# A long convolution inside a two-block model: transforms of half length over even and odd times

## The reference, cut to what matters

```python
h = jnp.sin(f1 * (z @ w1 + b1))
h = jnp.sin(f2 * (h @ w2 + b2))
h = h @ w3                                  # filters: 2 orders x 2 directions x 1024 channels
kern = concatenate([h_fwd, zeros(1), h_bwd[:0:-1]])      # after a decay window
kf = rfft(kern)

def long_conv(u, kf, bias):                 # u: 256 times x 1024 channels
    uf = rfft(u, n=512)
    return irfft(uf * kf, n=512)[:256] + u * bias

z   = hx1 * long_conv(hv, kf[order 0], bias[0])
y_a = hx2 * long_conv(z,  kf[order 1], bias[1])
```

## Time and profile before

| | |
|---|---|
| time, median of 3 runs | 2843.58 us (2842.61 to 2844.23) |
| the profiled execution's own time | 2843.16 us |
| its span, first to last instruction | 2840.9 us |
| PE busy | 2735.8 us (96%) |
| DVE busy | 1570.4 us (55%) |
| ACT busy | 1170.1 us (41%) |
| mean granted clock of PE | 0.985 |
| the Hyena mixer, from its first transpose to `br_b`'s first product | 1762.88 to 1884.55 us |

### The profile page before, as it was taken

The page is one execution under the profiler, slowest core; times in us unless marked ns, Lnnn a source line. Parts: engine busy times, 40 slices in busy tenths (PEclk is TensorE's granted clock), DMA queues, the critical chain, the costliest instruction groups (busy, mean ns, idle before and its releaser), DMA issues. The chain is left out here.

```text
span 2840.9 us, 53209 instructions
## 1 busy us (share of the span) xinstructions
PE 2735.8 (96%) x21454; PEld 2628.4 (93%) x21454; DVE 1570.4 (55%) x1868; ACT 1170.1 (41%) x1345; POOL 64.6 (2%) x59
## 2 busy tenths in 40 slices
PE   8999999999999999999999997989999999999998
PEld 8999898999988988999999994479999999999998
DVE  6445666564455665667654444556565555554443
ACT  5333465443343554433344442024354444443332
POOL 0000011010000000100000000000010000000000
PEclk9999999999999999999999997999999999999999
DMA  6555322545544334555555550025555555555553
GB/s 216 173 177 177 131 93 75 166 157 178 171 148 135 121 109 142 180 198 178 177 181 189 188 181 23 15 70 186 189 167 189 186 184 185 177 193 185 185 182 123
DMA packets 123699, 445.96 MB, mean 157 GB/s; under 512 B 13594, under 2 KB 15925, under 8 KB 123440
## 3 DMA queue, kind: packets, MB, share of 16 engines
q1 hardware_dynamic: 122208, 438.82, 47.0%
q0 software_dynamic: 1360, 5.27, 0.6%
HBM read 441.94 MB, written 2.10 MB: 156 GB/s over the span
## 5 line engine op out<-in xcount | busy, mean ns | idle before, releaser
L1611 PE MATMUL PS<-XH,hi 128*128 128x256 f32 (+1 forms) x5152 | 1466.0, 285 | 37.3 <-DVE lo L891 20.5
L1613 PE MATMUL PS<-XH,lo 128*128 128x256 f32 (+1 forms) x5152 | 1460.7, 284 | 0.0
L1612 PE MATMUL PS<-XL,hi 128*128 128x256 f32 (+1 forms) x5152 | 1460.1, 283 | 0.0
L891 DVE TENSOR_TENSOR lo<-raw,hi 128x1024 fp32r<-128x1024 f32 x728 | 898.8, 1249 | 853.9 <-ACT hi L467 842.7
L467 ACT ACTIVATE hi<-raw 128x1024 fp32r<-128x1024 f32 x728 | 762.0, 1057 | 1007.2 <-PE PS L1613 966.9
L1611 PEld LDWEIGHTS PS<-XH,hi 128*128 128x128 f32 x5152 | 975.1, 189 | 42.0 <-issue 28.4
L1612 PEld LDWEIGHTS PS<-XL,hi 128*128 128x128 f32 x5152 | 975.3, 189 | 0.1
L1613 PEld LDWEIGHTS PS<-XH,lo 128*128 128x128 f32 x5152 | 974.6, 189 | 0.0
L1673 PE MATMUL PS<-XH,hi 128*128 128x256 f32 (+1 forms) x768 | 229.4, 299 | 2.6 <-DVE XL L946 2.6
L1675 PE MATMUL PS<-XH,lo 128*128 128x256 f32 (+1 forms) x768 | 220.3, 287 | 0.0
L1674 PE MATMUL PS<-XL,hi 128*128 128x256 f32 (+1 forms) x768 | 219.7, 286 | 0.0
(11 more groups left out here) (329 smaller groups left out, 1602.9 us busy)
## 6 DMA issues: line engine op xcount, KB each, us to landing
raw<-stream SPq DMA_DIRECT2D x828, 512.0 KB, 3.6
H<-h_in SPq DMA_DIRECT2D x4, 544.0 KB, 8.2
y_win<-windows POOLq DMA_DIRECT2D x2, 1024.0 KB, 5.5
out<-H SPq DMA_DIRECT2D x4, 512.0 KB, 3.5
dftm<-dft POOLq DMA_DIRECT2D x1, 1024.0 KB, 5.8
w<-w POOLq DMA_DIRECT2D x2, 512.0 KB, 6.8
ml_m<-mask_ml POOLq DMA_DIRECT2D x1, 512.0 KB, 3.9
a_m<-masks_a POOLq DMA_DIRECT2D x1, 272.0 KB, 6.4
```

The source lines that it names most:

```text
L891: dve.tensor_tensor(lo[s][:, :], raw[s][:, :], hi[s][:, :].bitcast(F32), ALU.subtract)\
L1611: pe.matmul(PS[:, bank, 0:n], w_hi, x_hi, start=start, stop=False)
L1612: pe.matmul(PS[:, bank, 0:n], w_hi, x_lo, start=False, stop=False)
L1613: return pe.matmul(PS[:, bank, 0:n], w_lo, x_hi, start=False, stop=stop)
```

## The change

The transforms go to half length. Times are split into even and odd ones, 128 each, and the 256 bins into 128 low ones and their mirrors. The even times give a half spectrum A. Then the odd times are added in the same PSUM bank, which gives the low bins A + B. A mirror bin is A - B, and it is made as twice the even part less the sum: ACT copies A out (`first_half`) before the odd product starts, ACT copies the sum (`low_half`), and DVE makes 2A - (A + B) (`high_half`). Both spectra, of the filter and of the input, are now taken this way, so `spectra_product` reads SBUF only; it has two operations more, which form sum and difference over the mirrored bins (`y_Z`) for an inverse of half length. `y_back` has again 16 products, of 128 columns, and writes every second column of its bank.

The two directions of the filter are stacked in 128 rows: w3 lies with one direction in rows 0 to 63 and the other in rows 64 to 127, and `h2T` has a second copy with the lower rows negated, so that one product gives the sum and another the difference (`filter_rows` on DVE makes the rows, and zeroes the first time of the second direction). `windowed` is then two products with the window. The second layer of the filter's network works on 128 rows.

The units are reordered: `v % 2` is the half of the channels and `v // 2` the order. The first `y_filters` moves from ahead of the mLSTM's last part to behind the first turn, the windows come in one load, w3 in one load instead of two. In three places `root_read` moves PE's wait for the square root from chunk 5 of the product to chunk 7 (`kv`; `w2` and `gate_up` in the same way). The diff, cut to its core; of the removed functions, which are printed above, only some lines are kept:

```diff
+y_banks = {"input": 0, "sum": 2, "difference": 4, "filter": 4, "output": 6}
...
-    w3_halves = w3.rearrange("p (b h n) -> h p b n", h=2, n=512)
     gp.wait_ge(S("m_vt"), 4)
-    gp.dma_start(w3_0[:, :, :], w3_halves[0]).then_inc(S("w3_landed0"), 16)
+    gp.dma_start(y_w3[:, :, :], w3).then_inc(S("w3_landed"), 16)
     gp.wait_ge(S("m_num"), 2 * MH)
-    gp.dma_start(y_win[:, :, :, :], windows[:, :, :, 0:512]).then_inc(S("window_landed0"), 16)
-    gp.wait_ge(S("m_out"), MH)
-    gp.dma_start(w3_1[:, :, :], w3_halves[1]).then_inc(S("w3_landed1"), 16)
-    gp.wait_ge(S("y_windowed"), 4 * 2)
-    gp.dma_start(y_win[:, :, :, :], windows[:, :, :, 512:1024]).then_inc(S("window_landed1"), 16)
+    gp.dma_start(y_win[:, :, :, :], windows).then_inc(S("window_landed"), 16)
...
+        def turned(v):
+            act.wait_ge(S("y_ut"), v + 1)
+            if v:
+                act.wait_ge(S("y_us"), v)
+            act.activation(y_U[:, :, :], PS[:, 0:2, :], ACT.Copy).then_inc(S("y_u"), 1)
+        def first_half(name, dst, bank, v):
+            act.wait_ge(S(f"y_{name}A"), v + 1)
+            if v:
+                act.wait_ge(S("y_prod"), v)
+            act.activation(dst[:, :, 1, :], PS[:, bank:bank + 2, :], ACT.Copy).then_inc(S(f"y_{name}a"), 1)
+        def low_half(name, dst, bank, v):
+            act.wait_ge(S(f"y_{name}s"), v + 1)
+            act.activation(dst[:, :, 0, :], PS[:, bank:bank + 2, :], ACT.Copy).then_inc(S(f"y_{name}l"), 1)
         turned(0)
+        first_half("k", y_K, y_banks["filter"], 0)
+        first_half("u", y_V, y_banks["input"], 0)
+        low_half("k", y_K, y_banks["filter"], 0)
+        for v in range(4):
+            low_half("u", y_V, y_banks["input"], v)
+            if v < 3:
+                turned(v + 1)
+                first_half("k", y_K, y_banks["filter"], v + 1)
+                first_half("u", y_V, y_banks["input"], v + 1)
+                low_half("k", y_K, y_banks["filter"], v + 1)
+        act.wait_ge(S("y_prod"), 4)
         for k in range(4):
             src = (MO if k < 2 else HY)[:, 4 * (k % 2):4 * (k % 2) + 4, :]
+            if k >= 2:
+                act.wait_ge(S("y_out"), k + 1)
...
+    def filter_rows():
+        dve.wait_ge(S("f_sin"), 2)
+        upper = slice(FILT, P)
+        own(dve.memset(h2T[upper, 0, 0:1], 0.0))
+        own_last(dve.tensor_copy(h2T[0:FILT, 1, :], h2T[0:FILT, 0, :]))
+        own_last(dve.tensor_scalar(h2T[upper, 1, :], h2T[upper, 0, :], -1.0, None, ALU.mult))
+        own_wait()
+        dve.sem_inc(S("h2_ready"), 1)
...
+        def windowed(v):
+            if v == 0:
+                dve.wait_ge(S("window_landed"), 16)
+            else:
+                dve.wait_ge(S("y_ks"), v)
+            for part, bank in enumerate((y_banks["sum"], y_banks["difference"])):
+                dve.wait_ge(S("y_filt"), 4 * v + 2 * part + 2)
+                dve.tensor_tensor(y_F[:, part, :, :], PS[:, bank:bank + 2, :], y_win[:, v % 2, :, :], ALU.mult)\
+                    .then_inc(S("y_windowed"), 1)
+        def high_half(name, dst, bank, v):
+            dve.wait_ge(S(f"y_{name}a"), v + 1)
+            dve.wait_ge(S(f"y_{name}l"), v + 1)
+            own(dve.scalar_tensor_tensor(out=dst[:, :, 1, :], in0=dst[:, :, 1, :], scalar=2.0,
+                                         in1=PS[:, bank:bank + 2, :], op0=ALU.mult, op1=ALU.subtract),
+                f"y_{name}h", v + 1)
+        def spectra_product(v):
+            uc, us, kc, ks, t0, t1 = (t[:, i] for t in (y_V, y_K, y_T) for i in range(2))
+            own_last(dve.tensor_tensor(t0, uc, kc, ALU.mult))
+            own_last(dve.tensor_tensor(t1, us, ks, ALU.mult))
+            own_wait()
+            own_last(dve.tensor_tensor(t0, t0, t1, ALU.subtract))
+            own_last(dve.tensor_tensor(kc, us, kc, ALU.mult))
+            own_wait()
+            own(dve.tensor_tensor(t1, uc, ks, ALU.mult))
+            own(dve.tensor_tensor(t1, t1, kc, ALU.add), "y_prod", v + 1)
+            if v:
+                dve.wait_ge(S("y_inv"), v)
+            for part, op in enumerate((ALU.add, ALU.subtract)):
+                dve.tensor_tensor(y_Z[:, :, part, :], y_T[:, :, 0, :], y_T[:, :, 1, :], op).then_inc(S("y_z"), 1)
+        def gated(v):
+            half, o = v % 2, v // 2
...
+                                                  in1=PS[:, y_banks["output"] + j // 2,
...
         windowed(0)
+        for v in range(4):
+            high_half("k", y_K, y_banks["filter"], v)
+            high_half("u", y_V, y_banks["input"], v)
+            spectra_product(v)
+            if v < 3:
+                windowed(v + 1)
+            else:
                 for k in range(2):
                     lo_piece("branches", k, MO[:, 4 * k:4 * k + 4, :], SEQ)
+            gated(v)
...
-        if i < 4:
-            pe.wait_ge(S("rms_ready"), i + 1)
+    def root_read(i):
+        return lambda: pe.wait_ge(S("rms_ready"), i + 1)
...
+    product(prod["kv"], between={5: lambda: squares_sum(1, AB, T), 7: root_read(1)})
...
+    def y_filters(v):
+        if v == 0:
+            pe.wait_ge(S("w3_landed"), 16)
+            pe.wait_ge(S("h2_ready"), 1)
+        else:
+            pe.wait_ge(S("y_windowed"), 2 * v)
+            pe.wait_ge(S("y_kl"), v)
+            pe.wait_ge(S("y_kh"), v)
+        for part, bank in enumerate((y_banks["sum"], y_banks["difference"])):
             for k in range(2):
+                pe.matmul(PS[:, bank + k, :], h2T[:, part, k::2], y_w3[:, v // 2, 512 * (v % 2):512 * (v % 2) + 512],
+                          start=True, stop=True).then_inc(S("y_filt"), 1)
+    def y_even(bank, src):
+        for m in range(2):
+            ins = pe.matmul(PS[:, bank + m, :], dftm[:, m, 0, :], src[m][:, 0, :], start=True, stop=True)
         return ins
+    def y_odd(bank, src):
+        for m in range(2):
+            ins = pe.matmul(PS[:, bank + m, :], dftm[:, m, 1, :], src[m][:, 1, :], start=False, stop=True,
+                            skip_group_check=True)
+        return ins
+    y_filter = (y_F[:, 0], y_F[:, 1])
+    y_input = (y_U, y_U)
+    def y_filter_even(v):
+        pe.wait_ge(S("y_windowed"), 2 * v + 2)
+        y_even(y_banks["filter"], y_filter).then_inc(S("y_kA"), 1)
+    def y_filter_odd(v):
+        pe.wait_ge(S("y_ka"), v + 1)
+        y_odd(y_banks["filter"], y_filter).then_inc(S("y_ks"), 1)
+    def y_turn(v):
+        if v:
+            pe.wait_ge(S("y_ul"), v)
+            pe.wait_ge(S("y_uh"), v)
+        if v >= 2:
+            pe.wait_ge(S("y_out"), v - 1)
         for k in range(2):
             for j in range(4):
+                ins = pe.transpose(PS[:, y_banks["input"] + k, 128 * j:128 * j + 128],
+                                   HY[:, 4 * (v % 2) + j, k::2], ident)
         ins.then_inc(S("y_ut"), 1)
+    def y_input_even(v):
+        pe.wait_ge(S("y_u"), v + 1)
+        y_even(y_banks["input"], y_input).then_inc(S("y_uA"), 1)
+    def y_input_odd(v):
+        pe.wait_ge(S("y_ua"), v + 1)
+        y_odd(y_banks["input"], y_input).then_inc(S("y_us"), 1)
+    def y_back(v):
+        pe.wait_ge(S("y_z"), 2 * v + 2)
+        if v:
+            pe.wait_ge(S("y_out"), v)
         for j in range(4):
+            for k in range(2):
+                c0 = SEQ * (j % 2) + k
+                for m in range(2):
+                    ins = pe.matmul(PS[:, y_banks["output"] + j // 2, c0:c0 + SEQ - 1:2],
+                                    y_Z[:, m, k, 128 * j:128 * j + 128], dftm[:, 2 + m, k, :],
+                                    start=m == 0, stop=m == 1)
         ins.then_inc(S("y_inv"), 1)
...
-    y_filters(0)
...
+    y_filters(0)
+    y_filter_even(0)
+    y_input_even(0)
+    y_filter_odd(0)
+    for v in range(4):
+        if v < 3:
+            y_filters(v + 1)
+        y_input_odd(v)
+        if v < 3:
+            y_turn(v + 1)
+        y_back(v)
+        if v < 3:
+            y_filter_even(v + 1)
+            y_input_even(v + 1)
+            y_filter_odd(v + 1)
```

More of the change, by code:

```diff
@@ L294, in program @@
             MO = sb(ph, "MO", [P, HT, SEQ])
+            dftm = sb(ph, "dftm", [P, 4, 2, P])
             with ExitStack() as sub:
@@ L298, in program @@
                 ml_m = sb(sub, "ml_m", [P, 2, 2, SEQ])
-                dftm = sb(sub, "dftm", [P, 4, 2, SEQ])
                 m_C = sb(sub, "m_C", [P, 16])
             with ExitStack() as sub:
[L302 to L305, removed]
+                y_w3 = sb(sub, "y_w3", [P, 2, HW])
+                y_V = sb(sub, "y_V", [P, 2, 2, 512])
+                y_T = sb(sub, "y_T", [P, 2, 2, 512])
+                y_Z = sb(sub, "y_Z", [P, 2, 2, 512])
         with ExitStack() as ph:
@@ L513, in filter_sine @@
                 act.wait_ge(S("f_arg"), layer + 1)
-                act.activation(h2T[:, :] if layer else f_t[:, 1, :], f_t[:, 0, :], ACT.Sin)\
+                rows = slice(0, P if layer else FILT)
+                act.activation(h2T[:, 0, :] if layer else f_t[rows, 1, :], f_t[rows, 0, :], ACT.Sin)\
```

(15 more changed lines are left out.)

143 lines of the change are left out of this document (24 added, 119 removed).

## The result

| | before | after |
|---|---|---|
| median of 6 runs each, side by side | 2843.45 us (2842.61 to 2844.26) | 2855.41 us (2851.42 to 2856.49) |
| the profiled execution: time, span | 2843.16, 2840.9 us | 2856.04, 2854.0 us |
| mean granted clock of PE | 0.985 | 0.975 |
| first turn to `br_b`'s first product | 121.7 us | 128.8 us |

The change costs 11.96 us: the ratio is 1.0036, with a 95% interval of 1.0026 to 1.0046. The forecast was 2851.2 in a range of 2844 to 2860.

A forecast was written before the change was run, and what follows sets the result against it. The prediction took the mixer's closed round of waits between PE, ACT and DVE as the bound, no engine being full. Mixer +9.7 and roots -1.7 gave +8.0 on 2843.16: 2851.2 us, range 2844 to 2860.

The forecast's parts named there:

- The new round, 28.95 at the full clock: Hyena mixer, one unit from inverse to inverse: by its chain of waits 28.95 us, against 27.43 before the change.
- The clock ahead of the inverses, 4 x 1.7: PE, nearly idle ahead of each of the four inverses, starts them at a low clock: 1.7 us more each.
- The clock in the waits of 2.4 us, 3 x 1.7: PE's idle wait ahead of later filter values brings a clock drop all three times: 1.7 us more each.
- Rival 2: No clock drop in the three 2.4 us waits ahead of the filter values: 2846.1 us; chance 0.16.
- The start, 36.5: Start of the mixer up to the first inverse: terms together 36.5 us, so that inverse begins at 1799.4, before at 1794.96.
- The sum for the mixer, +9.7: Start, two rounds, third round and last inverse summed: the branch begins at 1894.2 us, 9.7 later than before.
- The signs: Expected in the profile: PE idle over 8 us ahead of inverses, DVE's high halves some 6.5 apart, no root waits.
- The roots, -1.7: Three waits of PE for ACT's square root, moved two chunks later, were to vanish: 1.7 us saved in all.
- `filter_rows`, w3, the windows at nothing: The new DVE rows, the single w3 load and the dropped second window load were to cost no time.
- Rival 1: The inverse's writes of every second column are slow: 1.7 us more on each of four, 2858 us; chance 0.27.
- That the clock stays up: Rival: PE keeps the full clock throughout, taking out 14.6 us: 2836.6 us, faster than before; chance 0.07.
- Rival 4: Time follows PE's work, about 10 us less per unit of the mixer: 2803 us; chance 0.04.

The follow-up runs named there:

- `e5_warm`: The changed kernel plus 42 products with unread results, ahead of inverses, later filter values and the last odd product: 2846.62 us, ratio 1.0001 to before.
- `e11_both`: The changed kernel with two units overlapped, first filter values early, unread products in PE's waits, and `kv`'s root wait put back: 2807.7 us, 0.9873 of before.

## Why the prediction was right, point by point

- *The bound.* Right. The mixer is a closed round of waits. 28 us less of PE's busy time gave +8.1 us; one exchange of two calls that adds and removes no work gave 2855.4 to 2833.9.
- *The new round, 28.95 at the full clock.* Right. With PE kept at work it is 29.4 and 29.2 (the inverses of `e5_warm` from 1802.52 to 1831.90 to 1861.05). DVE's product took 9.69 (1793.40 to 1803.09) for 9.65, the inverse 3.72 to 3.84 for 3.75, copy and high half fit. The input's high half in one round began 0.4 us late (1825.66) for a reason that the profile doesn't give.
- *The clock ahead of the inverses, 4 x 1.7.* Right in kind, too small: 8.7 in place of 6.8. The low stretches reached 4.9, 5.5, 4.5 and 3.4 us into the inverses, not 3.4 each, and half of that plus 3.7 gives, to 0.05 us, the 6.15, 6.45, 5.96 and 5.43 that the trace shows.
- *The clock in the waits of 2.4 us, 3 x 1.7.* Wrong in two of three. PE was idle 2.53, 2.57 and 2.57 us ahead of the filter values. Only the second brought a low stretch (5.38 us against 3.68, 3.68). The sum came out near since the inverses' error (+1.9) has the other sign, and that is luck. Rival 2 was thus two thirds right in its mechanism, and not in its time.
- *The start, 36.5.* From the first turn to the first inverse 35.9 was put and 33.4 measured: the first filter values took 4.57 in place of 5.73, the second lost nothing.
- *The sum for the mixer, +9.7.* Measured +8.1.
- *The signs.* PE stood idle 8.22, 8.46, 7.98 and 12.18 us ahead of the inverses, and DVE 6.7, 8.8 and 6.7 us between the two high halves, for over 8 and some 6.5. No wait for the root stands behind the sums.
- *The roots, -1.7.* This is the term that failed. Each of the three waits was taken as a loss of its own. That in `kv` was cover for a late chunk, and without it came the 2.0 us of idle at 629 us; with the two low stretches that go with it the three moves cost about 2 us.
- *Outside the mixer, nothing for the clock.* That missed what `kv`'s two low stretches cost, which the last point holds, and what the other places do by chance: the two near 493 and 514 us put the profile of the kernel after 2.9 us late where its work is the same.
- *Sum.* 8.1 + 2 is about 10, against 11.96 and 10.7 in two comparisons, and +8.0 forecast. That 2855.4 lies in the range is owed to the mixer's sum, which came out near with errors that cancel, and to a range wider than the root's error. What is left is within what chance in the low stretches makes: before itself went from 2839.4 to 2848.2 in 21 runs.
- *`filter_rows`, w3, the windows at nothing.* No wait on them shows in the trace after.
- *Rivals 1, 3 and 4.* Rival 1 is disproved. That the clock stays up did not happen by itself; made to happen within the mixer by added work, it gives 2846.6 and not 2836.6, since the mLSTM's last products ahead of the first turn and the first filter values still ran at a low clock, two of the added products stand in the chain for 1.72 us, and the part outside the mixer stays. Rival 4 is 52 us off.

The Trainium skill (PSUM — Partial Sum Buffer, Specifications) has non-contiguous access slowing matmuls significantly. For a write of every second fp32 column this case's traces do not agree: 6.12, 6.43, 5.95, 5.42 us with the stride and 6.12, 6.43, 5.96, 5.43 without. The measurement decides.

Not tried: the old transforms of full length in the overlapped order. What halving them is worth by itself stays open. The old unit's PE work alone is 7.17 + 3.63 + 1.04 + 7.15 and 7.08 for the filter's spectra, 26.1 us, so no order of it can reach the 19.8 of `e11_both`; that is argued from the sum, not measured.

## What to carry to other kernels

Where engines take turns in a closed round, write the round down from the new waits before counting the work saved, and look in each engine's order for work that the next engine doesn't need: here one exchange of two calls took off 21 us, more than the whole change had cost. A wait that is moved gains only if no later wait takes its time over, and an idle stretch of PE of 2 us is no small thing when it brings another 1.4 to 1.7 us by the clock. Once the order is right, less work can count: the halved transforms, 12 us slower as first placed, are part of a kernel 37.7 us faster than before.

## What the runs showed of the hardware that was not expected

- Work that is of no use made the kernel faster: 42 added products and 8.8 us less, by the granted clock of the inverses and of one call of the filter values.
- Idle stretches of PE of the same length at the same place bring a low clock in one execution and not in another (2.13 us at 492 us: in 12 of 14 profiles; 2.05 at 512: in 10 of 14). The time of one and the same kernel went over 9 us, in part by this: in the first session the runs of before with a mean clock of 0.986 took 2839.4 and 2840.6 us, those with 0.983 2846.2 to 2847.2; but the two slowest, 2847.8 and 2848.2, had 0.984, so the clock is not all of it.
- The same low stretch of 3.4 us cost 1.55 us near 493, 1.38 near 514 and nothing behind 2068, where PE would have waited for DVE as long.
- Whether the 2.1 us near 1067 us brings a low stretch went with an edit 440 us earlier in 13 of 14 profiles. What links the two is not shown.
- The Trainium skill (TensorE: Matmul & The Clock Gate, Part 1) says that the number of slow matmuls at a kernel's start varies from run to run. These traces agree: the changed kernel's two profiles have 22 and 18 slow products at the start (0.23 us from one to the next, 0.12 to 0.13 behind them). They show the same in the middle of a busy stream.
